# Norm factor moved behind the down projection, and eleven seven-product pairs in each of three FFNs

## The reference

```
h = x * rsqrt(mean(x*x, -1) + 1e-6) * norm_g
gate, up = split(h @ w_gu)            # 1024 -> 2 * 2816
x = x + 0.5 * (silu(gate) * up) @ w_down   # 2816 -> 1024
```

## Time and profile before

| what | us |
|---|---|
| median of 3 runs | 2204.29 |
| the profiled execution's own time | 2204.55 |
| its span, first to last instruction | 2202.8 |
| PE busy | 2186.0 (99%) |
| DVE busy | 1450.1 (66%) |
| ACT busy | 988.9 (45%) |
| POOL busy | 154.7 (7%) |
| granted TensorE clock, mean | 1.000 |

### The profile page before, as it was taken

One profiled execution on the slowest core, in us unless ns is written; L12 is line 12 of the kernel. 1 busy time (PEld: TensorE's weight loads), 2 busy tenths in 40 slices (PEclk: granted clock), 3 DMA queues, 4 the chain that ended last, 5 costly groups with the idle time before them and its releaser, 6 DMA issues.

```text
span 2202.8 us, 28606 instructions
## 1 busy us (share of the span) xinstructions
PE 2186.0 (99%) x11576; PEld 1780.6 (81%) x11576; DVE 1450.1 (66%) x2245; ACT 988.9 (45%) x1542; POOL 154.7 (7%) x127
## 2 busy tenths in 40 slices
PE   9999999999999999999999999999999999999999
PEld 7889897777778898988898887777788888877777
DVE  6757476988657574766576677777575536555863
ACT  5424234667444242335333236777442222238672
POOL 3000003000120000030000021000310000020000
PEclk9999999999999999999999999999999999999999
DMA  6323234131225232232323232222144334242211
GB/s 196 115 77 115 77 104 131 40 97 59 77 76 193 79 110 82 96 115 77 115 93 118 87 105 78 79 75 85 58 153 143 125 115 134 92 133 77 77 58 39
DMA packets 201604, 217.77 MB, mean 99 GB/s; under 512 B 4777, under 2 KB 194345, under 8 KB 201473
## 3 DMA queue, kind: packets, MB, share of 16 engines
q1 hardware_dynamic: 194768, 193.48, 27.2%
q0 software_dynamic: 6560, 22.39, 3.0%
q10 hardware_dynamic: 144, 0.08, 0.0%
HBM read 213.79 MB, written 6.32 MB: 100 GB/s over the span
## 4 chain that ended last, share of the span: by engine, by line
PE 91%; DVE 5%; ACT 3%; issue 1%; DMA 0%; POOL 0%; SPq 0%; DVEq 0%; ACTq 0%
PE ps L1829 90%; DVE sb_wlo L1230 1%; PE ps L1833 1%; ACT sb_whi L715 1%; DVE sb_gla_ek L1535 0%; DVE sb_gla_eq L1538 0%; DMA sb_xT<-xT 0%; ACT sb_xh L715 0%; DVE sb_xT L1334 0%; ACT sb_hyb_th L715 0%; DVE sb_gla_xb L1530 0%; DVE sb_gla_cf L1527 0%; DVE sb_gla_d L1515 0%; DVE sb_xl L1252 0%; ACT sb_lnb L715 0%
## 5 line engine op out<-in xcount | busy, mean ns | idle before, releaser
L1829 PE MATMUL ps<-sb_xh,sb_whi 128*128 128x512 f32 (+1 forms) x2016 | 771.0, 382 | 1.8 <-DVE sb_xl L1618 0.9
L1829 PE MATMUL ps<-sb_xl,sb_whi 128*128 128x512 f32 (+1 forms) x2016 | 753.3, 375 | 0.3 <-DVE sb_xl L1252 0.3
L1829 PE MATMUL ps<-sb_xh,sb_wlo 128*128 128x512 f32 (+1 forms) x2016 | 751.2, 375 | 0.0
L715 ACT ACTIVATE sb_whi<-sb_raw 128x1024 fp32r<-128x1024 f32 (+1 forms) x376 | 378.3, 1016 | 411.0 <-PE ps L1829 403.7
L1230 DVE TENSOR_TENSOR sb_wlo<-sb_raw,sb_whi 128x1024 fp32r<-128x1024 f32 (+1 forms) x328 | 408.7, 1251 | 207.7 <-ACT sb_whi L715 205.0
L1829 PEld LDWEIGHTS ps<-sb_xh,sb_whi 128*128 128x128 f32 x2016 | 379.7, 188 | 86.5 <-issue 18.1
L1829 PEld LDWEIGHTS ps<-sb_xl,sb_whi 128*128 128x128 f32 x2016 | 380.0, 188 | 70.6 <-DVE sb_xl L1252 3.4
L1829 PEld LDWEIGHTS ps<-sb_xh,sb_wlo 128*128 128x128 f32 x2016 | 379.5, 188 | 69.5
L1829 PE MATMUL ps<-sb_ffn_ah,sb_whi 128*128 128x512 f32 x704 | 274.3, 390 | 0.0
L1829 PE MATMUL ps<-sb_ffn_ah,sb_wlo 128*128 128x512 f32 x704 | 273.9, 389 | 0.0
L1829 PE MATMUL ps<-sb_ffn_al,sb_whi 128*128 128x512 f32 x704 | 273.9, 389 | 0.0
(11 more groups left out here) (295 smaller groups left out, 2521.6 us busy)
## 6 DMA issues: line engine op xcount, KB each, us to landing
sb_raw<-ffn_w_gu SPq DMA_DIRECT2D x86, 1024.0 KB, 5.1
sb_raw<-ffn_w_down SPq DMA_DIRECT2D x32, 1024.0 KB, 5.4
sb_raw<-gla_w_in SPq DMA_DIRECT2D x12, 1024.0 KB, 5.4
sb_raw<-diff_w_in SPq DMA_DIRECT2D x12, 1024.0 KB, 5.1
sb_ada_raw<-w_ada POOLq DMA_DIRECT2D x12, 1024.0 KB, 6.3
sb_raw<-w_in SPq DMA_DIRECT2D x10, 1024.0 KB, 5.3
sb_raw<-ffn_w_down SPq DMA_DIRECT2D x12, 768.0 KB, 4.5
sb_raw<-gla_w_out SPq DMA_DIRECT2D x4, 1024.0 KB, 5.6
```

The costliest lines, as they stand in the source:

```text
L715: return e.activation(out, in_, func, bias=bias, scale=scale)
L1829: return e.matmul(out, lhsT, rhs, start=start, stop=stop, skip_group_check=skip)
```

## The change

It has four parts.

- The up tile is no longer multiplied by `rb`. A plain pair forms `psum_up * gate` directly, and its second bank is emptied by `f_p`, where it was `f_u`. A fast pair leaves out the multiplication at the end of `join_halves`. The factor is put in where a down product is added to x: first `gb = psum * 0.5 * rb` (signal `f_t`), then, after a wait for it, `x = x + gb` (signal `f_x`). Down banks are emptied by `f_t`. This holds for all four FFNs.
- The x sums get a tile of their own (`x_sum`), which lies where the second half of `al` (the low parts of the products) will be, so that `weight_sums` and the copy of the first product no longer wait for the end of the x sums.
- `FAST` has 11 pairs in each of FFN 0, 1 and 2: 4, 6, 8, 9, 11, 12, 14, 16, 17, 19, 20. Four times in an FFN, one fast pair is now followed by another only one place later (8 and 9, 11 and 12, 16 and 17, 19 and 20).
- In FFN1 the tiles `onehot` and `bias_rows` lie over `ah`, and the wait for `bias_vec` goes from DVE (j = 6) to ACT (j = 4).

```diff
-FAST = (tuple(range(6, 22, 2)),) * 3 + ((),)
+FAST = ((4, 6, 8, 9, 11, 12, 14, 16, 17, 19, 20),) * 3 + ((),)
...
+            with ExitStack() as early:
+                x_sum[f] = sb(f"ffn{f}_xs", [128, 8, 256], F32, early)
+            al += tiles_of(sb(f"ffn{f}_al4", [128, 4, S], F32R, mem))
...
-                            w.wait_ge(sem["t_vec"], 4 * t_before[f + 1])
                             act(first_product(sums, i), psum[FFN_NORM][:, 256 * (i % 2):256 * (i % 2) + 256],
...
-                            scaled_x(f, j, sums)
+                            scaled_x(f, j, x_sum[f])
...
                         w.wait_ge(sem["f_p"], J + 1)
+                        if f == 1 and j == 4:
+                            w.wait_ge(sem["bias_vec"], 16)
                         act(ah[:, j - k0, :], ub[j % 2][:, :], ACT.Copy).then_inc(sem["f_ah"], 1)
...
-                w.wait_ge(sem["t_vec"], 4 * t_before[ffn_of(u) + 1])
                 lo_done(w, u - 1)
                 e.tensor_tensor(sums[:, 0:4, :], c_, d_, ALU.add).then_inc(sem["s_add"], 1)
...
-                            e.tensor_tensor(v, psum[banks[1]][:, :], rb[:, :], ALU.mult).then_inc(sem["f_u"], 1)
...
-                        w.wait_ge(sem["f_u"], J + 1)
-                        if f == 1 and j == 6:
-                            w.wait_ge(sem["bias_vec"], 16)
                         if fast:
+                            w.wait_ge(sem["f_join"], 4 * (fast_before[f] + FAST[f].index(j)) + 4)
                             e.scalar_tensor_tensor(out=v, in0=v, scalar=-1.0, in1=g, op0=ALU.mult,
                                                    op1=ALU.mult).then_inc(sem["f_p"], 1)
                         else:
-                            e.tensor_tensor(v, v, g, ALU.mult).then_inc(sem["f_p"], 1)
+                            e.tensor_tensor(v, psum[banks[1]][:, :], g, ALU.mult).then_inc(sem["f_p"], 1)
...
-                        e.scalar_tensor_tensor(out=x[:, m, :], in0=psum[f_banks[f]["down", (part, m)][0]][:, :],
-                                               scalar=0.5, in1=x[:, m, :], op0=ALU.mult,
-                                               op1=ALU.add).then_inc(sem["f_x"], 1)
+                        e.scalar_tensor_tensor(out=gb[m % 2], in0=psum[f_banks[f]["down", (part, m)][0]][:, :],
+                                               scalar=0.5, in1=rb[:, :], op0=ALU.mult,
+                                               op1=ALU.mult).then_inc(sem["f_t"], 1)
+                        w.wait_ge(sem["f_t"], part_x(f, part, m))
+                        e.tensor_tensor(x[:, m, :], x[:, m, :], gb[m % 2], ALU.add).then_inc(sem["f_x"], 1)
...
-                w.wait_ge(sem["f_join"], 4 * i + 4)
-                e.tensor_tensor(up, up, rb[:, :], ALU.mult).then_inc(sem["f_u"], 1)
...
-                            emptied[banks[0]], emptied[banks[1]] = ("f_g", J + 1), ("f_u", J + 1)
+                            emptied[banks[0]], emptied[banks[1]] = ("f_g", J + 1), ("f_p", J + 1)
...
-                        emptied[b] = "f_x", part_x(f, part, m)
+                        emptied[b] = "f_t", part_x(f, part, m)
```

More of the change, by code:

```diff
@@ L385 @@
 x_hi x_lo sq sq_first sq_add sq_last norm lnb warm
-f_g f_silu f_u f_p f_ah f_al f_x out_x
+f_g f_silu f_t f_p f_ah f_al f_x out_x
 s_add t_act t_vec f_join
@@ L421, in build, with tiles_of @@
         bias_rep = nc.dram_tensor("bias_rep", (8, 128 * 1024), F32).ap()
+        x_sum = {}
+        def tiles_of(t):
+            return [t[:, k, :] for k in range(t.shape[1])]
         def ffn_memory(f, mem):
             if not FAST[f]:
-                return (sb(f"ffn{f}_ah", [128, 12, S], F32R, mem), sb(f"ffn{f}_al", [128, 12, S], F32R, mem),
+                return (sb(f"ffn{f}_ah", [128, 12, S], F32R, mem), tiles_of(sb(f"ffn{f}_al", [128, 12, S], F32R, mem)),
                         [sb(f"ffn{f}_g{i}", [128, S], F32, mem)[:, :] for i in range(2)],
                         [sb(f"ffn{f}_u{i}", [128, S], F32, mem) for i in range(2)], None, None, None, None)
-            ah, al = sb(f"ffn{f}_ah", [128, 8, S], F32R, mem), sb(f"ffn{f}_al", [128, 8, S], F32R, mem)
+            ah, al = sb(f"ffn{f}_ah", [128, 8, S], F32R, mem), tiles_of(sb(f"ffn{f}_al", [128, 4, S], F32R, mem))
+            with ExitStack() as early:
+                x_sum[f] = sb(f"ffn{f}_xs", [128, 8, 256], F32, early)
+            al += tiles_of(sb(f"ffn{f}_al4", [128, 4, S], F32R, mem))
             vgw = [sb(f"ffn{f}_vgw{i}", [128, 4, 256], F32, mem) for i in range(2)]
@@ L516, in build @@
         first_squares = rb[:, :], lnb[:, :], ffn_mem[0][3][1][:, :]
-        def tiles_of(t):
-            return [t[:, k, :] for k in range(t.shape[1])]
         XH, XL = tiles_of(xh), tiles_of(xl)
@@ L793, in ffn @@
                             w.wait_ge(sem["t_vec"], 4 * (t_before[f] + j) + 3)
-                            act(th[:, j, :, :], sums[:, 8:16, :], ACT.Copy).then_inc(sem["t_act"], 1)
+                            act(th[:, j, :, :], x_sum[f][:, 4:8, :], ACT.Copy).then_inc(sem["t_act"], 1)
                     last = part == len(parts) - 1
@@ L808, in ffn, with scaled_x @@
                             act((sq, rb)[m - KT + 2][:, :], x[:, m, :], ACT.Square).then_inc(sem["sq_last"], 1)
-            def scaled_x(f, t, sums):
-                y = sums[:, 0:8, :].rearrange("p (k c) d -> p k (c d)", k=2)
+            def scaled_x(f, t, xs):
+                y = xs[:, 0:4, :].rearrange("p (k c) d -> p k (c d)", k=2)
                 if t:
@@ L1307, in ffn @@
                         else:
-                            e.tensor_tensor(v, v, g, ALU.mult).then_inc(sem["f_p"], 1)
+                            e.tensor_tensor(v, psum[banks[1]][:, :], g, ALU.mult).then_inc(sem["f_p"], 1)
                         if FAST[f] and j < 4:
                             w.wait_ge(sem["t_act"], t_act_before[f] + 3 * j + 3)
-                            e.tensor_tensor(tl[:, j, :, :], sums[:, 8:16, :],
+                            e.tensor_tensor(tl[:, j, :, :], x_sum[f][:, 4:8, :],
                                             th[:, j, :, :].bitcast(F32), ALU.subtract).then_inc(sem["t_vec"], 1)
@@ L1339, in ffn, with x_sums @@
                             x_lo(NORM_OF_FFN[f] + 1, m)
-            def x_sums(f, t, sums):
+            def x_sums(f, t, xs):
                 n = t_before[f] + t
-                y = sums[:, 0:8, :].rearrange("p (k c) d -> p k (c d)", k=4)
-                out = sums[:, 8:16, :].rearrange("p (k c) d -> p k (c d)", k=4)
+                y, out = xs[:, 0:4, :], xs[:, 4:8, :]
                 w.wait_ge(sem["t_act"], t_act_before[f] + 3 * t + 2)
```

8 lines of the change are left out of this document (4 added, 4 removed).

## The result

The changed kernel takes 2261.99 us (median of 4 runs, 2260.98 to 2263.67) against 2204.35 us for the kernel before (4 runs on the same chip, 2204.25 to 2204.54): ratio 1.0262, 95% interval 1.0250 to 1.0274. It is slower by 57.6 us. The forecast was 2258.0 us in a range of 2232 to 2270. All medians are of fast executions; one execution of the first experiment, 6864 us, is a slow one and left out.

A forecast was written before the change was run, and what follows sets the result against it. It took PE's instruction stream to bound the kernel. Terms: 2204.55 − 7.4 (stream) + 23.8 (pair 4) + 14.5 (pairs in a row) + 17.8 (exits) + 5 (clock) = 2258.2, so 2258 us, range 2232 to 2270.

The forecast's parts named there:

- The stream of PE: In FFN0 to 2, more fast pairs shorten PE's matmul stream by 2.46 us each, −7.4 us in all.
- The moved factor: Leaving the factor out of the up tile saves DVE 0.60 us per plain pair, by itself worth 0.
- Pair 4: In FFN0, 1 and 2 PE waits for the late fourth `tl`: 8.1, 7.3 and 8.3 us, +23.8 us.
- PE waits on DVE `ffn_tl`: Sign in the trace after: such a wait of 5 to 7 us, once in each of FFN0, 1 and 2, inside pair 4.
- Two fast pairs in a row: At pairs 12 and 20 of three FFNs PE waits 1.25 us (first join) and 1.2 (low weights): +14.5 us.
- The exits: Behind FFN0, 1 and 2 the added DVE instruction delays x: +5.0, +7.2, +4.9, and 0.7 in FFN3, together +17.8 us.
- The clock: About six stops of 4.5 to 7 us slow PE's clock afterwards: 5 us taken, ends 0 and 13.
- The rival that the clock falls at every stop: The clock drops to 1.2 GHz at every stop, each return costing 2.2 us: 2266 us, chance 0.20.
- All covered: Rival: x sums and FFN-end rounds are in time, only PE's stream and a final 0.7 us count: 2197.6 us, chance 0.08.
- only the exits: Rival: pair 4 and fast pairs in a row cost nothing, the FFN exits' loop remains: 2214.7 us, chance 0.06.
- The exits hidden: Rival: the added steps behind the down products are hidden and nothing else is: 2235 us, chance 0.04.

The follow-up runs named there:

- the first experiment: The changed kernel with the old choice of fast pairs (6, 8, 10 to 20), the norm's factor still moved: 2224.41 us.
- the last run: The kernel of "all of it" with the norm's factor on the up tile in all parts: 2197.19 us, ratio 0.9967 to the kernel before.
- filled waits: The changed kernel with 28 matmuls whose result nobody reads added in pair 4 of FFN0 and of FFN2: 2258.73 us.
- ScalarE's order: The changed kernel with two ACT instructions (copy of `th`, rounding of the next pair's first weights) moved ahead of its wait for `f_p`: 2233.54 us.
- no pair 4: The changed kernel with pair 4 plain again, the other ten fast pairs kept: 2234.28 us.
- none in a row: The changed kernel with fast pairs 4, 6, 8, 10 to 20, so no two stand in a row: 2251.09 us.
- last part as before: The changed kernel with factor on the up tile and one-instruction addition to x in the last part of FFN0 to 2 and in FFN3: 2242.34 us.
- all of it: The changed kernel with pair 5 fast instead of 4, "ScalarE's order", "last part as before", and FFN2's bank ring begun at 1: 2197.14 us.

## Why the prediction was right, point by point

*The stream of PE, −7.4 us:* right. Unhindered fast pairs take 10.07 us as before, and the two kernels without stops are 7.2 us faster.

*The moved factor is worth 0 inside the pairs:* right; the run with it alone shows no gain, and the last run loses nothing without it.

*Pair 4, 8.1 + 7.3 + 8.3 us:* right within 0.1 in FFN0 and FFN2, where the clock is taken out. The fourth `tl` in FFN0 was forecast for 65.71 + 0.55 = 66.26 and starts at 66.10. The run with filled waits measures the stop as 8.2 us in FFN0 and 8.4 in FFN2 (18.45 − 10.07). A part of each is a wait that the forecast didn't name, for the low weights (2.21 and 2.41 us), so that the waits for `tl` are 5.46 and 4.63.

In FFN1 the sign "PE waits on DVE `ffn_tl`" did not come. PE waits for `bias_rows` alone, before pair 4, and not within it (rows of PE's and DVE's timelines of the change):

```profile
690.30 0.55 PE L1831 MATMUL ps<-sb_xh,sb_whi 128*128 128x256 f32 x1 [5.63 <-DVE sb_bias_rows L1291]
...
694.40 1.23 DVE L1314 TENSOR_TENSOR sb_ffn_tl<-sb_ffn_xs,sb_ffn_th 128x1024 fp32r<-128x1024 f32 x1 [1.64 <-ACT sb_ffn_th L721]
...
696.16 0.28 PE L1831 MATMUL ps<-sb_ffn_th,sb_whi 128*128 128x256 f32 x1
```

By the prediction's own terms this `tl` is usable at 694.40 + 1.40 = 695.8, and at full clock PE would have wanted it at 690.30 + 3.96 = 694.3. That is an estimate of 1.5 us for the second wait, with 5.8 for the first the 7.3 forecast. At half clock PE came to it only at 696.16: its slow matmuls ran in place of the wait, and stop and clock together are 7.7 us.

*Two fast pairs in a row, 14.5 us:* right, 6 × 2.33 = 14.0, in the two pieces foretold. The first join held pair 12 back until 194.07, where it would have started at 182.63 + 10.07 = 192.70: 1.37 us for a forecast 1.25. The low weights took the other 0.96 us, for 1.2.

*The exits, 17.8 us:* right. Rounds of 4.96 and 5.2 were forecast, and 4.96 and 5.22 are read. The stop before FFN2 was put at 7.2, and PE's wait there is 6.95 us, 7.1 on the stage. Behind FFN0 the stage grew by 7.2 us and behind FFN2 by 7.2, for 5.0 and 4.9: these 2.2 and 2.3 us more are the clock's, as both stages run at 0.50 there. From the end of FFN1 to pair 4 of FFN2 PE took 1057.5 − 1003.7 = 53.8 us for 1018.4 − 973.9 = 44.5 before, 9.3 more for a stop of 7.1, so 2.2 are the clock's there.

*The clock, 5 us:* the mechanism right, the size wrong. This is the step that failed, in the prediction's words "There will be about six stops of 4.5 to 7 us. Ends 0 and 13; I take 5". The runs give the cost by subtraction. The sum of the other terms (sizes as forecast where the traces agree, 14.0 for the pairs in a row, 9.5 for pair 4 with ScalarE's order) is taken from each run's median and from its profiled execution. The stretches of half clock are counted in the latter:

| run | sum without the clock | median | rest | profiled | rest | low stretches |
|---|---|---|---|---|---|---|
| the change | 2252.6 | 2262.0 | 9.4 | 2263.7 | 11.1 | 6 |
| factor alone | 2219.8 | 2224.4 | 4.6 | 2225.5 | 5.7 | 3 |
| no pair 4 | 2228.9 | 2234.3 | 5.4 | 2234.8 | 5.9 | 3 |
| none in a row | 2241.1 | 2251.1 | 10.0 | 2251.5 | 10.4 | 6 |
| filled waits | 2252.8 | 2258.7 | 5.9 | 2258.8 | 6.0 | 4 |
| last part as before | 2237.6 | 2242.3 | 4.7 | 2241.0 | 3.4 | 3 |
| ScalarE's order | 2224.3 | 2233.5 | 9.2 | 2235.9 | 11.6 | 6 |
| all of it | 2197.0 | 2197.1 | 0.1 | 2197.0 | 0.0 | 0 |

By the medians a stretch costs 1.5 to 1.8 us on average, by the profiled executions, in five of the seven kernels the longest of theirs, 1.1 to 2.0. Single ones differ more. In the change's profile, read as above, pair 4 lost 2.6, 0.4 (7.7 − 7.3) and 1.6 us to the clock in FFN 0, 1 and 2, and the exits 2.2, 2.2 and 2.3. So the start of the kernel's 2.2 per return was a fair size for a stretch whose slow matmuls nothing hides; too low was the number of returns to be paid. I had discounted six stops to about two, and in the profile all six had half clock. The rival that the clock falls at every stop was right on where, and a little too dear: 2266 for a measured 2262.0. The error of the whole forecast, 4.0 us, is this term (9.4 for 5) less the 0.5 for the pairs in a row.

The Trainium skill (TensorE: Matmul & The Clock Gate, "What's actually happening") knows two states of the clock, 1.2 GHz as the idle one and 2.4 GHz reached by work. The windows above agree, with 0.50 behind the stop and 1.00 later, and so does the run with filled waits, in which the engine had work and the clock never fell there.

*The rivals on the other side.* "All covered" and "only the exits" fell with the `tl` at 66.10: DVE's queue there was as unbroken as the rows said. "The exits hidden" fell with the 19.9 us of the factor alone.

## What to carry to other kernels

An engine that is busy for two thirds of the time can still make another wait everywhere, when its results go through a second engine and come back: here 28.5 us hung on where two of ACT's instructions stand in its queue, and none on the step that had been taken off DVE. Before work is saved on an engine, look for the idle time inside its chain (a bracket such as 1.65 us behind a result of its own) and who stands ahead of the one that ends it. An instruction added to a loop that already runs late, as at the FFN's end, is paid once per round (seven rounds and the last result, 4.96 us), however idle the engine is on average, and a long stop of the tuned stream can cost the clock's return as well, as the six of the change did.

## What the runs showed of the hardware that was not expected

In the change half clock came with each of the six long stops (the shortest wait was 3.33 us), and with ScalarE's order even with one of 2.00 us, while at the pairs of waits at 12 and 20 (1.21 and 0.63 us) the clock stayed at 1.00. The length of the wait alone doesn't decide it: with the last part as before, PE waited for 2.66 us ahead of FFN2, and the clock stayed at 1.00. Why it fell at the shorter one and not at this is not shown.

What a stretch cost, 0.4 to 2.6 us in the change's profile, did not follow the length of the stop (the exit with a wait of 6.95 us lost 2.2 us, the one with 4.25 us lost 2.3). In FFN1 part of it was hidden by a wait that it replaced. A matmul of 128x512 took 0.43 us at the granted 0.50 for 0.227 at 1.00, and one of 128x256 took 213 ns for 120 (24 steps from 67.98 to 73.10 us). And 28 matmuls that compute nothing made the pair in which they stand 2.6 us faster in FFN0 and 1.6 us in FFN2.
